# Light units in runs of four, one gather for two light experts, and column halves at the end of an expert

## The chip, the cores and the metric

The kernel runs on one core of one Trainium2 chip. The metric is the device time of one execution in microseconds. A core has TensorE (PE, matmuls; PEld is its weight load), VectorE (DVE), ScalarE (ACT), GpSimd (POOL) and SyncE (SP), and 16 DMA engines that move data between its memory SBUF and HBM. Matmuls write to PSUM, eight banks of 512 float32 columns.

## The reference

Two decoder layers over 256 tokens of width 1024 in float32. Each adds a mixer (differential attention and retention, gated) and then an FFN. In layer 0 the FFN is dense, in layer 1 it is a mixture of eight SwiGLU experts of which each token uses two:

```python
for e in range(N_EXPERTS):
    out = out + combine[:, e:e + 1] * ((silu(t @ w1[e]) * (t @ w3[e])) @ w2[e])
```

with `t = rms_norm(h)`, the top two of the router's logits and a softmax over them for `combine`. An expert's weights are 1024 x 2816 twice and 2816 x 1024: 34.6 MB; all eight 277 MB.

## The kernel before

The weights come as **units** of 128 x 2048 float32 (1.049 MB). The mixers and the dense FFN load them one by one. An expert has 33 units: 22 gate units (`w1` and `w3`; a slice of 512 hidden columns takes four units) and 11 down units (two chunks of 128 hidden rows by 1024 columns each). They are loaded in pairs, 2.1 MB in one DMA, the last one alone: 17 loads per expert, 136 in all (`LOADS`).

**Two kinds of experts.** The experts are put in order of how many tokens they have, counted on the chip. Four places (`CHAIN`) are computed densely for up to 128 tokens: each unit is split by ScalarE (`split_hi`, line 598) and VectorE (`split_lo`, line 616) into a high and a low part, and `product` (lines 621 to 623) makes three matmuls of each tile, 12 per unit with 512 columns. Four places (`SMALL`, the **light** experts, up to 64 tokens) skip the split: `few_halves` (line 1728) multiplies float32 directly, two column halves side by side in the array. A dense unit takes more TensorE time, a light one less, and both bring the same bytes. `moe_orders` mixes the two, so that TensorE and DMA keep step: after each dense load it lets in light loads that are due. `LOADED` is the order of the transfers, `TAKEN` the order of use; a light load is used before the dense load that was fetched just ahead of it. `FEW_ALONE` is the number of light units meant to come after all dense ones.

**The ring.** Loads go to a ring of five places of 2.1 MB. SyncE issues load i when load i-5 has left its place (`load_ring`, line 562, DMAs on lines 578 and 580): a dense one when its last unit is split, a light one when TensorE has used it. Splits run two units ahead of TensorE.

**Gathers.** Tokens of an expert are gathered by matmuls with a one-hot matrix `sel`, made on VectorE (`chain_select`, `few_select`). `gather_rows` (line 1612) does it for a dense expert with 128 places, `few_gather_rows` (line 1624) for one light expert with 64. They read `hn`, the normed rows, which `normed_rows` (line 1104) makes from `xs` on ScalarE just after the first dense unit. Only the first gather (line 1600) reads `xs` and has the norm `rn` in `sel`. Before it `keep_busy_wide` has TensorE multiply spare data, at its end three strided matmuls (line 1547).

**The results.** The rows of each expert but the last light one are stored to HBM in `y_rows` (line 800 and `few_store_rows`). When the last dense rows are stored, GpSimd fetches each token's rows by index (line 825) and VectorE adds them to `h` (`add_rows`, line 2401). The last light expert isn't stored: ScalarE copies its result out of PSUM (line 1189), TensorE spreads it over the tokens (`few_scatter`, line 1796), VectorE adds it (`few_add`, line 2462), and three DMAs write the output (lines 741, 743 and 1247).

Of the kernel before, what the change touches and what calls it, by code (L numbers as in the profile page):

```python
# [31 lines left out]
P = 128  # L32
# [42 lines left out]
FEW_FROM, FEW_ALONE = 6, 12  # L75
# [8 lines left out]
def moe_orders():  # L84
# [97 lines left out]
def build(nc, x, boot_d, positions, units_d, pairs_d, lasts_d, zeros_d, cols_d, rows_d, out):  # L182
    ctx = ExitStack()
    with ctx:
# [27 lines left out]
        few_X = over("few_X", KC * FEW)[:, :].rearrange("p (c n) -> p c n", c=KC)  # L212
# [5 lines left out]
        y_back_rows = over("y_back_rows", D)  # L218
# [10 lines left out]
        back.append(y_back_rows)  # L229
# [10 lines left out]
        raw = sb("raw", [P, RAW, UNIT])  # L240
        wh = sb("wh", [P, SPLIT, UNIT], F32R)
        wl = sb("wl", [P, SPLIT, UNIT], F32R)
# [3 lines left out]
        hn = nc.alloc_sbuf_tensor_at("hn", [P, TT * D], F32, offset=xt_at + 4 * 2 * KC * P)  # L246
# [8 lines left out]
        back.append(cols[:, COLS_LAST:COLS_LAST + D])  # L255
# [151 lines left out]
        y_first = sem("y_first")  # L407
# [21 lines left out]
        hn_rows = sem("hn_rows")  # L429
# [41 lines left out]
        TURNED, FEW_TURNED, FEW_ROWS, FEW_DOWN = 4, 5, 2, 3  # L471
        FEW_SUMS = (0, 1, 6, 7)
# [275 lines left out]
        def _(pool):  # L748
# [47 lines left out]
            def store_rows(p, e):  # L796

                pool.wait_ge(y_cp, 2 * l_no(p) + 2)
                pool.wait_ge(y_sent, 16 + 16 * l_no(p))
                pool.dma_start(rows_in(y_d, Y_ZERO, e), xs3[:, 0, :]).then_inc(y_sent, 16)  # L800

            def few_store_rows(p, e):
# [28 lines left out]
        def _(act):  # L831
# [265 lines left out]
            def normed_rows():  # L1097

                act.wait_ge(rs_ready, 2 * ROOTS)
                for n in range(2):  # L1100
                    act.wait_ge(hg_ready, n + 1)
                    for t in range(TT):
                        at = slice(t * D + n * 512, t * D + (n + 1) * 512)
                        ins = nc.scalar.activation(hn[:, at], xs[:, at], ACT.Copy, scale=rn[:, t:t + 1])
                    ins.then_inc(hn_rows, 1)

# [12 lines left out]
            def few_rows_whole(p):  # L1119

                act.wait_ge(few_rows_tr, few_no(p) + 1)
                nc.scalar.activation(few_X[:, :, :], ps[:, FEW_ROWS, :].rearrange("p (c n) -> p c n", c=KC), ACT.Copy)\
                    .then_inc(few_rows, 1)
# [41 lines left out]
            def few_unit(p, U, j):  # L1165
# [12 lines left out]
                if u == 8 and few_no(p) + 1 < len(SMALL):  # L1178
                    few_rows_whole(SMALL[few_no(p) + 1])
                if u == 6 and p == SMALL[-1]:  # L1180
                    act.wait_ge(few_sel_tr, 1)
                    nc.scalar.activation(selT[:, 0:SEQ], ps[:, TURNED, 0:SEQ], ACT.Copy).then_inc(few_sel_cp, 1)
                if u == SLICES - 1:
                    if few_no(p) > 0:
                        act.wait_ge(few_sent, 32 * few_no(p))
                    act.wait_ge(unit_used, U.count(j))
                    for n in range(2):
                        at = slice(256 * n, 256 * n + 256)
                        nc.scalar.activation(xs3[:, 1, at], ps[:, FEW_DOWN, at], ACT.Copy).then_inc(few_y, 1)

            def large_unit(p, U, j, scatter=None):
# [20 lines left out]
                if then is not None:  # L1212
                    split_hi(act, *then)
                if u == SLICES - 1:
# [3 lines left out]
                    act.wait_ge(y_first, l_no(p) + 1)  # L1218
                    nc.scalar.activation(xs3[:, 0, 0:512], ps[:, banks[0], :], ACT.Copy).then_inc(y_cp, 1)
                    act.wait_ge(unit_used, U.count(j))  # L1220
                    nc.scalar.activation(xs3[:, 0, 512:D], ps[:, banks[1], :], ACT.Copy).then_inc(y_cp, 1)
# [29 lines left out]
        def _(pe):  # L1251
# [243 lines left out]
            def down_unit(pe, U, j, outs, gT, u, halves=None):  # L1495
# [4 lines left out]
                steps = [(a, n) for a in range(2) for n in range(2)]  # L1500
                if halves is not None:
                    steps.sort(key=lambda step: step[1])
                for a, n in steps:
                    b = slice(a * D + n * 512, a * D + (n + 1) * 512)
                    for banks, t in outs:
                        last = product(ps[:, banks[n], :], gT[0][:, 2 * u + a, t], gT[1][:, 2 * u + a, t],
                                       wh[:, s, b], wl[:, s, b], u == 0 and a == 0, u == SLICES - 1 and a == 1)
                    if halves is not None and (a, n) == (1, 0):
                        last.then_inc(halves, 1)
# [28 lines left out]
            def keep_busy_wide():  # L1538
# [47 lines left out]
            def gather(sels):  # L1586
# [3 lines left out]
                of = xs if routing else hn  # L1590
# [1038 lines left out]
```

## Time and profile before

| | |
|---|---|
| median of 3 runs | 1219.03 us (1218.44 to 1220.32) |
| profiled execution | 1219.02 us, its span 1217.2 us |
| busy: PE, DVE, ACT, POOL | 1202.1, 737.4, 593.7, 67.8 us |
| moved by DMA | 384.8 MB |
| expert stage | from about 550 us to the end |

An engine's busy time over the span says how full it is on average, not what sets the end. Times in rows are microseconds from the start of the span. Where several matmuls stand in one row, the duration runs from the first start to the last end, and matmuls overlap: what counts is the distance of the starts.

### The profile page before, as it was taken

The page shows a single profiled execution, that of the slowest core. Times are in us where ns is not written, and L with a number is a line of the kernel's source. Part 1 is how long each engine was busy: PE and PEld are TensorE (multiplying, and loading weights), DVE is VectorE, ACT ScalarE, POOL GpSimd, SP SyncE. Part 2 cuts the span into 40 slices and gives each one's busy share as a digit, 9 for nine tenths or more (in the row PEclk, how much of TensorE's full clock was granted, in tenths as well). Part 3 has the DMA queues.
Part 4 walks back from the last instruction along what each step waited for, and adds up shares of the span by engine and source line. Part 5 has one row for each costly group of instructions (what it writes and reads, how often), then busy time and mean ns, then how long its engine had stood idle before and what let it go on. Part 6 is the DMA issues. An engine that isn't in the chain of part 4 may idle for free.

```text
span 1217.2 us, 15724 instructions
## 1 busy us (share of the span) xinstructions
PE 1202.1 (99%) x6377; PEld 907.8 (75%) x6377; DVE 737.4 (61%) x769; ACT 593.7 (49%) x645; POOL 67.8 (6%) x55
## 2 busy tenths in 40 slices
PE   9999999999999999999999999999999999999996
PEld 8778888888888888888777666777567776667762
DVE  6867766656445857767665745755546664566532
ACT  6667435444436467446545434544535444454430
POOL 0600001000000600000000000000000000000001
PEclk9999999999999999999999999999999999999999
DMA  9753558555554454367999999999999999999997
GB/s 378 302 197 117 182 184 295 184 202 178 184 197 173 169 177 141 136 248 275 408 425 428 385 424 416 428 428 418 424 416 430 427 421 415 427 429 426 429 423 299
DMA packets 36590, 384.82 MB, mean 316 GB/s; under 512 B 4337, under 2 KB 4337, under 8 KB 7985
## 3 DMA queue, kind: packets, MB, share of 16 engines
q1 hardware_dynamic: 34672, 374.83, 76.8%
q0 software_dynamic: 1696, 8.66, 1.9%
q8 instruction: 53, 0.87, 0.3%
q10 hardware_dynamic: 144, 0.26, 0.1%
q14 instruction: 25, 0.20, 0.0%
HBM read 379.80 MB, written 7.61 MB: 318 GB/s over the span
## 4 chain that ended last, share of the span: by engine, by line
PE 91%; DMA 2%; DVE 2%; issue 2%; ACT 1%; POOL 1%; SPq 0%; DVEq 0%; ACTq 0%; POOLq 0%
PE ps L621 22%; PE ps L623 21%; PE ps L622 21%; PE ps L1728 18%; PE ps L1254 3%; DMA ring<-in_pairs 1%; PE ps L1624 1%; DMA h<-in_x 1%; PE ps L1612 1%; DVE wl L616 1%; POOL rst L759 1%; PE ps L1313 1%; ACT wh L598 0%; PE ps L1600 0%; DVE mix L2088 0%
## 5 line engine op out<-in xcount | busy, mean ns | idle before, releaser
L616 DVE TENSOR_TENSOR wl<-raw,wh 128x2048 fp32r<-128x2048 f32 x170 | 391.9, 2307 | 259.8 <-ACT wh L598 259.2
L598 ACT ACTIVATE wh<-raw 128x2048 fp32r<-128x2048 f32 x170 | 325.4, 1917 | 262.5 <-PE ps L623 243.6
L621 PE MATMUL ps<-wh,XT 128*128 128x512 f32 x856 | 341.7, 399 | 1.2 <-DVE wl L616 1.1
L623 PE MATMUL ps<-wh,XT 128*128 128x512 f32 x856 | 333.8, 390 | 0.0
L622 PE MATMUL ps<-wl,XT 128*128 128x512 f32 x856 | 333.6, 390 | 0.0
L621 PEld LDWEIGHTS ps<-wh,XT 128*128 128x128 f32 x856 | 160.7, 188 | 52.2 <-issue 16.2
L623 PEld LDWEIGHTS ps<-wh,XT 128*128 128x128 f32 x856 | 160.7, 188 | 34.5
L622 PEld LDWEIGHTS ps<-wl,XT 128*128 128x128 f32 x856 | 160.9, 188 | 30.9
L616 DVE TENSOR_TENSOR wl<-ring,wh 128x2048 fp32r<-128x2048 f32 x48 | 109.9, 2290 | 79.5 <-ACT wh L598 79.2
L598 ACT ACTIVATE wh<-ring 128x2048 fp32r<-128x2048 f32 x48 | 91.9, 1914 | 101.7 <-PE ps L623 90.8
L1728 PE MATMUL ps<-raw,few_X 128*64 128x256 f32 x768 | 88.2, 382 | 0.0
L1728 PEld LDWEIGHTS ps<-raw,few_X 128*64 128x64 f32 x768 | 53.0, 137 | 31.4 <-issue 7.2
L1728 PE MATMUL ps<-ring,few_X 128*64 128x256 f32 x640 | 73.5, 382 | 0.0
L621 PE MATMUL ps<-wh,moe_gT_h 128*128 128x512 f32 x176 | 71.2, 405 | 0.0
L623 PE MATMUL ps<-wh,moe_gT_l 128*128 128x512 f32 x176 | 68.7, 390 | 0.0
L622 PE MATMUL ps<-wl,moe_gT_h 128*128 128x512 f32 x176 | 68.7, 390 | 0.0
L1728 PEld LDWEIGHTS ps<-ring,few_X 128*64 128x64 f32 x640 | 44.3, 137 | 25.9 <-issue 5.8
L1728 PE MATMUL ps<-raw,few_gT 128*64 128x512 f32 x208 | 48.9, 600 | 0.1
L621 PEld LDWEIGHTS ps<-wh,moe_gT_h 128*128 128x128 f32 x176 | 33.1, 188 | 10.8 <-issue 3.9
L923 ACT ACTIVATE mix<-ps,rn 128x512 f32<-128x512 f32 x40 | 26.0, 688 | 27.2 <-PE ps L623 27.1
L623 PEld LDWEIGHTS ps<-wh,moe_gT_l 128*128 128x128 f32 x176 | 33.0, 188 | 7.2
L622 PEld LDWEIGHTS ps<-wl,moe_gT_h 128*128 128x128 f32 x176 | 33.1, 188 | 6.1
(296 smaller groups left out, 1151.9 us busy)
## 6 DMA issues: line engine op xcount, KB each, us to landing
raw<-in_pairs SPq DMA_DIRECT2D x76, 2048.0 KB, 13.1
ring<-in_pairs SPq DMA_DIRECT2D x52, 2048.0 KB, 13.5
raw<-in_units SPq DMA_DIRECT2D x86, 1024.0 KB, 4.9
raw<-in_lasts SPq DMA_DIRECT2D x6, 1024.0 KB, 13.6
y_rows<-in_zeros POOLq DMA_DIRECT2D x7, 512.0 KB, 7.9
raw<-in_boot SPq DMA_DIRECT2D x5, 512.0 KB, 7.1
y_rows<-xs POOLq DMA_DIRECT2D x4, 512.0 KB, 10.9
ring<-in_lasts SPq DMA_DIRECT2D x2, 1024.0 KB, 10.9
```

Source lines behind the costliest of these rows:

```text
L598: nc.scalar.activation(wh[:, U.split_slot(j), :], U.raw(j), ACT.Copy).then_inc(hi_ready, 1)
L616: nc.vector.tensor_tensor(wl[:, s, :], U.raw(j), wh[:, s, :].bitcast(F32), ALU.subtract).then_inc(lo_ready, 1)
L621: nc.tensor.matmul(o, xh, bh, start=start, stop=False)
L622: nc.tensor.matmul(o, xh, bl, start=False, stop=False)
L623: return nc.tensor.matmul(o, xl, bh, start=False, stop=stop)
L759: nc.gpsimd.tensor_tensor(to, of, nhalf[:, 0:of.shape[-1]], ALU.pow).then_inc(rs_ready, 1)
L923: ins = nc.scalar.activation(to, acc, ACT.Copy if g < 6 else ACT.Sigmoid, scale=rn[:, t:t + 1])
L1254: return nc.tensor.transpose(o, i, ident)
L1313: last = nc.tensor.matmul(ps[:, (6, 6, 4)[k] + c, a * n:(a + 1) * n], qkT[part, hd, tok[t]], qkT[part, 4 + hd, 0:n], start=True, stop=True)
L1612: last = nc.tensor.matmul(ps[:, rows_bank(p) + n, a * P:(a + 1) * P], hn[:, at:at + P], sel[:, t * SEQ:t * SEQ + P], start=t == 0 and a == ...
L1624: last = nc.tensor.matmul(ps[:, FEW_ROWS, c * FEW:(c + 1) * FEW], hn[:, at:at + P], sel[:, t * SEQ + P:t * SEQ + P + FEW], start=t == 0 an ...
L1728: last = nc.tensor.matmul(o[at], x, of[half], start=start, stop=stop, tile_position=(0, half * FEW))
```

## The change

- `moe_orders` lets light loads in two at a time, so that a run of light work is four units (three where an expert's single last unit is among them), and `FEW_ALONE` goes from 12 to 16.
- `few_select` and `few_gather_rows` serve two light experts at once, in 64 of 128 places each; two gathers in place of four.
- `hn` and `normed_rows` are gone. All gathers read `xs`, and `rn` is multiplied into the one-hot matrices. The results that lay in `xs` go to a tile `ys` in the place of `hn`. One split of the opening comes ahead of the first copies of gathered rows on ScalarE.
- The three strided matmuls of `keep_busy_wide` are gone.
- The last two units of each expert hold the last four chunks by column halves, so that one half of the columns is finished a unit earlier. The last light expert uses two PSUM banks, and its copy, spread and add go half by half. `few_store_rows` stores the same rows in pieces of 256 columns.

```diff
-FEW_FROM, FEW_ALONE = 6, 12
+FEW_FROM, FEW_ALONE = 6, 16
...
-        while due - done >= few[0][2]:
-            loaded.append(few[0])
-            taken.insert(len(taken) - 1, few[0])
-            done += few.pop(0)[2]
+        while due - done >= few[0][2] + few[1][2]:
+            for _ in range(2):
+                loaded.append(few[0])
+                taken.insert(len(taken) - 1, few[0])
+                done += few.pop(0)[2]
...
+        FEW_ROWS = (2, 5)
+        FEW_SUMS = ((0, 6), (2, 4))
+        def few_down_banks(p):
+            return (3, TURNED) if p == SMALL[-1] else (3, 3)
...
-                for n in range(2):
-                    pool.dma_start(rows_in(y_d, Y_ZERO, e)[0:FEW, n * 512:(n + 1) * 512],
-                                   xs3[n * FEW:(n + 1) * FEW, 1, 0:512]).then_inc(few_sent, 16)
+                for half in range(2):
+                    to = rows_in(y_d, Y_ZERO, e)[0:FEW, :].rearrange("r (n h d) -> r h n d", n=2, h=2)[:, half]
+                    of = ys[half * FEW:(half + 1) * FEW, 1, 0:512].rearrange("p (n d) -> p n d", n=2)
+                    pool.dma_start(to, of).then_inc(few_sent, 16)
...
-            def normed_rows():
...
-                if (p, j) == (0, 1):
-                    normed_rows()
+            split_hi(act, *ahead_of(units_of(0), 0))
             gathered_hi(0)
...
+            def down_half_unit(pe, U, j, banks, gT, n):
+                pe.wait_ge(lo_ready, U.splits(j))
+                s = U.split_slot(j)
+                for a in range(4):
+                    c, b = FC - 4 + a, slice(a * 512, (a + 1) * 512)
+                    last = product(ps[:, banks[n], :], gT[0][:, c, 0], gT[1][:, c, 0], wh[:, s, b], wl[:, s, b], False, a == 3)
+                last.then_inc(unit_used, 1)
...
-                for _ in range(3):
-                    nc.tensor.matmul(ps[:, 4, :].rearrange("p (t b n) -> p t b n", t=2, n=16), x,
-                                     w.rearrange("p (b t n) -> p t b n", t=2, n=16), start=True, stop=True)
...
             def few_gather_rows(p):
-                pe.wait_ge(hn_rows, 2)
-                pe.wait_ge(few_sel, few_no(p) + 1)
-                for t in range(TT):
-                    for c in range(KC):
-                        at = t * D + c * P
-                        last = nc.tensor.matmul(ps[:, FEW_ROWS, c * FEW:(c + 1) * FEW], hn[:, at:at + P],
-                                                sel[:, t * SEQ + P:t * SEQ + P + FEW], start=t == 0 and c == 0,
-                                                stop=t == TT - 1 and c == KC - 1)
-                last.then_inc(few_rows_tr, 1)
+                pe.wait_ge(few_sel, few_no(p) // 2 + 1)
+                for n in range(2):
+                    for t in range(TT):
+                        for a in range(4):
+                            at = t * D + (4 * n + a) * P
+                            last = nc.tensor.matmul(ps[:, FEW_ROWS[n], a * P:(a + 1) * P], xs[:, at:at + P],
+                                                    sel[:, t * SEQ + P:(t + 1) * SEQ], start=t == 0 and a == 0,
+                                                    stop=t == TT - 1 and a == 3)
+                    last.then_inc(few_rows_tr, 1)
...
+                for n in range(2):
+                    pe.wait_ge(few_y, 2 * len(SMALL) - 1 + n)
+                    for t in range(TT):
+                        for half in range(2):
+                            at = slice(half * FEW, (half + 1) * FEW)
+                            last = nc.tensor.matmul(ps[:, FEW_SUMS[n][t] + half, n * 256:(n + 1) * 256], selT[at, tok[t]],
+                                                    ys[at, 1, n * 256:(n + 1) * 256], start=True, stop=True)
+                        last.then_inc(few_sum[n], 1)
```

## Rows read from the trace of the kernel before

**Rows 1.** The page's busy times over the whole span.
```profile
PE 1202.1 (99%) x6377; PEld 907.8 (75%) x6377; DVE 737.4 (61%) x769; ACT 593.7 (49%) x645; POOL 67.8 (6%) x55
```

**Rows 2.** Stretches: PE, PEld, DVE, ACT, POOL busy, PE clock, DMA share, GB/s.
```profile
660.00:680.00 20.00, 20.00 (x129) 15.18 (x129) 12.09 (x28) 10.46 (x9) 0.00 (x0) 1.00 0.94 384
680.00:700.00 20.00, 19.31 (x89) 12.73 (x85) 13.18 (x24) 8.93 (x9) 0.00 (x0) 1.00 0.99 406
...
800.00:820.00 20.00, 20.00 (x127) 14.68 (x127) 12.80 (x14) 9.24 (x9) 0.00 (x0) 1.00 1.01 429
...
900.00:920.00 20.00, 20.00 (x106) 12.58 (x106) 10.97 (x7) 8.92 (x10) 1.07 (x2) 1.00 0.99 409
...
1000.00:1020.00 20.00, 20.00 (x130) 14.30 (x128) 11.14 (x10) 8.69 (x7) 0.00 (x0) 1.00 0.99 403
```

**Rows 3.** SyncE's waits from 600 to 1190: for whom, us, times, longest.
```profile
SPq L578 <- DVE wl L616: 383.7, 60, 10.7
```

**Rows 4.** The seventeenth load and the last one: issue, and time to landing.
```profile
L578 SPq DMA_DIRECT2D ring<-in_pairs x1: 328/328/328, 610.5 to 610.5; - x1
...
DMA to landing us min/median/max: 12.6/12.6/12.6
...
L580 SPq DMA_DIRECT2D raw<-in_lasts x1: 332/332/332, 1189.0 to 1189.0; - x1
...
DMA to landing us min/median/max: 15.6/15.6/15.6
```

**Rows 5.** Timeline: start, duration, engine, line. One round, and two light loads in succession.
```profile
1150.04 3.67 PE L1728 MATMUL ps<-raw,few_X 128*64 128x256 f32 x32
...
1154.44 0.40 PE L621 MATMUL ps<-wh,moe_gT_h 128*128 128x512 f32 x1
...
1158.53 0.39 PE L621 MATMUL ps<-wh,moe_gT_h 128*128 128x512 f32 x1
...
1159.30 3.67 PE L1728 MATMUL ps<-raw,few_X 128*64 128x256 f32 x32
...
1188.60 3.60 PE L1728 MATMUL ps<-ring,few_gT 128*64 128x512 f32 x16
...
1192.04 3.60 PE L1728 MATMUL ps<-raw,few_gT 128*64 128x512 f32 x16
```

**Rows 6.** Groups on TensorE: the four light and three dense gathers (busy, mean ns).
```profile
L1624 PE MATMUL ps<-sel,hn 128*128 128x64 f32 x128 | 15.0, 276 | 0.0
...
L1612 PE MATMUL ps<-sel,hn 128*128 128x128 f32 x96 | 11.3, 276 | 0.0
```

**Rows 7.** The opening of the expert stage: timeline rows, and TensorE's longest wait.
```profile
545.04 0.89 PE L1547 MATMUL ps<-wh,MT_h 128*128 128x512 f32 x3
...
545.77 0.29 PE L1579 MATMUL ps<-routed,cols 128*128 128x16 f32 x2
...
553.23 2.55 ACT L1104 ACTIVATE hn<-xs,rn 128x512 f32<-128x512 f32 x4
...
PE ps L621 <- DVE wl L616: 0.9, 1, 0.9
```

**Rows 8.** The end: timeline, a row of the chain of waits, and one stretch.
```profile
1184.60 16.16 DMA ring<-in_pairs
...
1192.77 1.05 POOL L825 DMA_INDIRECT back<-y_rows,yidx  x1 [10.13 <-DMA y_rows<-xs]
...
1204.66 1.94 PE L1728 MATMUL ps<-raw,few_gT 128*64 128x512 f32 x8
...
1207.90 1.28 DVE L2401 SCALAR_TENSOR_TENSOR h<-cols,tw,h 128x1024 f32<-128x1024 f32 x1
...
1209.40 2.73 DVE L2462 SCALAR_TENSOR_TENSOR h<-ps,comb,h 128x512 f32<-128x512 f32 x4 [0.22 <-DVE h L2401]
...
1212.16 0.38 ACTq L1247 DMA_DIRECT2D out<-h  x1
...
1204.50:1210.00 5.50, 3.97 (x18) 1.35 (x16) 4.45 (x4) 0.66 (x2) 0.00 (x0) 1.00 0.27 101
```

More of the change, by code:

```diff
@@ L1211, in large_unit @@
                 then = ahead_of(U, j)
-                if then is not None:
+                if then is not None and not (scatter is None and (p, j) == (0, 0)):
                     split_hi(act, *then)
@@ L1493, in dense, with down_unit @@
                         last.then_inc(down_half, 1)
-            def down_unit(pe, U, j, outs, gT, u, halves=None):
+            def down_unit(pe, U, j, outs, gT, u):
                 pe.wait_ge(lo_ready, U.splits(j))
                 s = U.split_slot(j)
[L1500 to L1509, printed above, removed]
+                for a in range(2):
+                    for n in range(2):
+                        b = slice(a * D + n * 512, a * D + (n + 1) * 512)
+                        for banks, t in outs:
+                            last = product(ps[:, banks[n], :], gT[0][:, 2 * u + a, t], gT[1][:, 2 * u + a, t],
+                                           wh[:, s, b], wl[:, s, b], u == 0 and a == 0, u == SLICES - 1 and a == 1)
+                last.then_inc(unit_used, 1)
[5 more added lines that the diff above has]
+                    last = product(ps[:, banks[n], :], gT[0][:, c, 0], gT[1][:, c, 0], wh[:, s, b], wl[:, s, b], False, a == 3)
                 last.then_inc(unit_used, 1)
@@ L1589, in gather @@
                 routing = isinstance(sels, int)
-                of = xs if routing else hn
                 if not routing:
@@ L1593, in gather @@
                 for n in range(2):
-                    pe.wait_ge(*((hg_ready, n + 1) if routing else (hn_rows, n + 1)))
+                    if routing:
+                        pe.wait_ge(hg_ready, n + 1)
                     for t in range(TT):
@@ L1758, in few_down_unit @@
                 j = 2 * SLICES + u
-                pe.wait_ge(few_lo, few_done(p, u // 2))
+                n = u - (SLICES - 2)
+                pe.wait_ge(few_lo, few_done(p, u // 2 if n < 0 else WIDE))
                 pe.wait_ge(*U.landed(j))
-                w = U.raw(j).rearrange("p (a n d) -> p a n d", a=2, n=2)
-                for a in range(2):
-                    last = few_halves(ps[:, FEW_DOWN, :], few_gT[:, 2 * u + a, :], [w[:, a, n] for n in range(2)],
-                                      u == 0 and a == 0, u == SLICES - 1 and a == 1)
+                banks = few_down_banks(p)
+                if u == 0 and p == SMALL[-1]:
+                    pe.wait_ge(y_cp, 2 * len(CHAIN))
+                if n < 0:
+                    w = U.raw(j).rearrange("p (a n h d) -> p a h n d", a=2, n=2, h=2)
+                    for a in range(2):
+                        x, first = few_gT[:, 2 * u + a, :], u == 0 and a == 0
+                        if banks[0] == banks[1]:
+                            o = ps[:, banks[0], :].rearrange("p (n d) -> p n d", n=2)
+                            last = few_halves(o, x, [w[:, a, half] for half in range(2)], first, False)
+                        else:
+                            for m in range(2):
+                                o = ps[:, banks[m], m * 256:(m + 1) * 256]
+                                last = few_halves(o, x, [w[:, a, half, m] for half in range(2)], first, False)
+                else:
+                    w = U.raw(j).rearrange("p (a h d) -> p a h d", a=4, h=2)
+                    for a in range(4):
+                        last = few_halves(ps[:, banks[n], n * 256:(n + 1) * 256], few_gT[:, FC - 4 + a, :],
+                                          [w[:, a, half] for half in range(2)], False, a == 3 and (n == 1 or banks[0] != banks[1]))
                 last.then_inc(unit_used, 1)
@@ L1791, in few_scatter @@
                 pe.wait_ge(y_cp, 2 * len(CHAIN))
[L1792 to L1797 removed]
+                for n in range(2):
+                    pe.wait_ge(few_y, 2 * len(SMALL) - 1 + n)
[5 more added lines that the diff above has]
+                        last.then_inc(few_sum[n], 1)
             gather(1)
@@ L2569, in ffn @@
                 unit([np.concatenate([w1[half * 4 + c][:, at], w3[half * 4 + c][:, at]], 1) for c in range(4)])
-        for c in range(0, FC, 2):
+        for c in range(0, FC - 4 if wide else FC, 2):
             unit([w2[c][:, 0:512], w2[c][:, 512:D], w2[c + 1][:, 0:512], w2[c + 1][:, 512:D]])
+        if wide:
+            for n in range(2):
+                unit([w2[c][:, n * 512:(n + 1) * 512] for c in range(FC - 4, FC)])
     mixer(0)
```

133 lines of the change are left out of this document (61 added, 72 removed).

## The prediction

> **What bounds the kernel now.** I read the page first. TensorE is busy 99% of the span [rows 1], which looks like a TensorE-bound kernel; but ends of matmuls are modelled, so this alone decides nothing. The second view is the table of stretches over the expert stage [rows 2]. What to see there: TensorE is full, and at the same time the 16 DMA engines are full, and the rate never passes about 429 GB/s. The third view, SyncE's own waits, says who paces the loads: SyncE waits for a ring slot nearly all the time [rows 3], so a transfer starts when TensorE (or the split on VectorE) frees a slot. Both engines are thus close to their limit, and the question is which is late at the end.
>
> Landing times settle it. The seventeenth load, issued at 610.5, took 12.6 us and was there at 623.1; the last one, issued at 1189.0, took 15.6 and was there at 1204.6 [rows 4]. Between them lie 230 units of 1.049 MB, at 429 GB/s 2.446 us each: 563 us. The rest of the traffic in that time (four row stores of 0.52 MB, three of 0.26, about 1.5 of the 2.1 MB of the final row gathers, 0.5 MB of instructions) is 4.9 MB or 11.4 us. Full speed would have ended at 1197; the stream came in 7.6 us later. Where that went, the stretches show: 384, 406, 409 and 403 GB/s instead of 429 in four stretches of 20 us are 2.1, 1.1, 0.9 and 1.2 us, 5.3 in sum [rows 2]. All four lie where one expert gives way to the next, that is beside a gather of rows on TensorE. There TensorE frees slots too late and the DMA engines run dry. So the last landing is set by bytes plus the time lost to a late TensorE, and behind it comes a tail of 12.6 us.
>
> **TensorE's saving.** A round of one light and one dense load ran from 1150.04 to 1159.30, 9.26 us [rows 5]. The dense matmuls inside are 18 starts in 4.09 us (1154.44 to 1158.53), 0.227 each, so 24 cost 5.45. Two light units back to back cost 3.44 (1188.60 to 1192.04). The remainder, 0.37 us, is the price of changing between light and dense work, there and back. Writing out both orders gives 59 such rounds before and 29 after (29 runs of four or three light units): 30 x 0.37 = 11.1 us saved. A gather for one light expert (128 matmul records with 64 columns) costs 3.75 us, the one for a dense expert with 128 columns 3.77 [rows 6]; columns do not count here, so one shared gather costs what a single one did, and two of four vanish: 7.5 us. Light units left for after the dense work go from 13 to 19 (loads go in pairs, so sixteen becomes nineteen): 6 x 1.72 = 10.3 us leave the dense stretch. In the opening, three strided matmuls stand ahead of the routing matmuls (0.7 us from their start to that of the next [rows 7]), and the 2.55 us of scaled copies on ScalarE delay a split for which TensorE waits 0.9 us [rows 7]; both go away, the second because rn now sits in the one-hot factors and one split moves into idle time. TensorE would so reach the end of dense work 1.6 + 11.1 + 7.5 + 10.3 = 30 us sooner if data were always there. They are not.
>
> The added operations are cheap. The shared selection is still four VectorE instructions; the copy of shared rows is two ScalarE instructions in place of one; light results now go out in pieces of 1 KB. The last two units of each dense expert hold the same 24 products. The last light expert writes two banks with twice the matmuls at half the columns, the form in which gate units already run at the same 1.72 us. I cost all these at nothing: ScalarE and VectorE do them under a light run of 6.9 us, and uncovered they would cost at most their own length, 0.64 us for 512 columns on ScalarE (2.55 for four [rows 7]), twice.
>
> **What of it reaches the end.** TensorE alone would end the dense work at about 1180 - 30 = 1150. The last dense load lands 19 units (46.5 us) and the last store and the row gathers (2.6 MB, 6.1 us) before the last landing; with that at about 1200, as found below, it is 1147. The two are level now, where before TensorE was the later one. So saved TensorE time pays only where the stream starved or started late. Terms, against the last landing at 1204.6:
> (a) Start. Slots are freed by TensorE's progress. At least its 1.6 us come through. The seventeenth load waits, by the rule of load i-5, for the fourth light load in both orders, with 14 dense and eight light units of work ahead of its slot; the changes on that way fall from 3.5 rounds to 1.5, 0.7 us more. I take 2.3, and twice the 0.7 as the upper bound, 3.1, since the loads in between move too.
> (b) Starvation. Of 5.3 us visible, from nothing to all may come back. The first handover comes after only five rounds, too early for much lead; the later ones find TensorE ahead. I take 3.5.
> (c) Final row gathers. Now they are issued from 1192.8 on [rows 8], in the way of the last two loads, and part of their bytes moves after the last landing: 101 GB/s over 5.5 us from 1204.5 on [rows 8], 0.55 MB. With 19 light units behind the dense work, all is done before. Their bytes then lie ahead of the last load: +1.3 us.
> The last landing moves by -2.3 - 3.5 + 1.3 = -4.5 us.
> The Trainium skill (DMA: Bandwidth & Descriptors, "Issuing engines are not separate DMA queues") says that transfers issued from GpSimd and SyncE share the same 16 DMA engines and interleave. By that rule (c) is a cost, as I take it; with separate paths it would be zero and the sum 1.3 us lower.
>
> (d) Tail. Before: last unit 1204.66 to 1206.60, copy, four sums; VectorE is busy adding gathered rows until 1209.18 and starts the light adds at 1209.40; last store issued 1212.16, and the span ends 5.0 us later [rows 8]. After: the gathered rows are in long before, and the first half of the columns is copied while the second is computed, so the first add starts some 0.6 us behind TensorE's last product instead of 2.8; against this, the last load will land only 2.45 us behind the pair before it (3.8 now: 1184.60 + 16.16 against 1204.6 [rows 4, 8]), whose two units take 3.44, so TensorE ends up to 1.0 us later against the landing. Net 1.2 to 2.2 saved, I take 1.7.
>
> Sum: -4.5 - 1.7 = -6.2 us. The profiled execution took 1219.02, its span 1217.2, the median of the runs is 1219.03, so there is nothing to correct: 1212.8 us.
>
> **The rivals.**
> Starvation stays (0.14): longer runs of light units free two slots at once and then none for a long dense stretch, so the handovers stay as dry as they are. Term (b) is 0, the time 1216.3.
> Lumpy slots starve the stream (0.08, the one on the other side). Each run of four leaves some 11 us of dense work in which slots come free only by splits. Now the queue holds two to three loads (12 to 17 us of landing time at 4.9 each), which speaks against it. If each of the 29 rounds lost 0.3 us of stream, that would be 8.7 us and eat the whole gain; from 0.3 on it is a loss, and with 0.5 the time is 1227.
> More comes back (0.14): all starvation, and the whole 3.1 of the start: -3.1 - 5.3 + 1.3 - 2.2 = -9.3, 1209.7.
> The clock falls (0.04): after the dense work TensorE has 3.44 us of work for each 4.9 us of stream and idles 1.5 us per load, nine times. The granted clock stayed at 1.00 in the stretch from 1204.5 to 1210, although TensorE was busy for only 3.97 of its 5.5 us [rows 8]. If it fell to its lower level, the last unit and sums would take twice their 4 us: 1216.8. The Trainium skill (TensorE: Matmul & The Clock Gate, "What's actually happening") holds that idleness throttles the clock; no row shows it for waits this short.
> The change does nothing (0.04): something else, such as 1 KB store pieces or instruction fetches, takes what was won: 1219.
>
> **Numbers.** The forecast itself has 0.56, own range 1211 to 1215. A measurement of this kernel can tell about 0.2%, 2.4 us. Faster by more: forecast, "more", and six in ten of "starvation stays": 0.78. Within: 0.14. Slower: 0.08. The 8-in-10 range: down to the better case with its bounds, 1209.0, up past "starvation stays" with the weaker tail (1.2) and start (1.6), 1217.5.
>
> **What the profile after should show.** TensorE waiting for DMA several times after the dense work, none of it in the opening; dense work ending between 1148 and 1158; the stretches at the handovers near 425 GB/s; the last landing at about 1200; the row gathers issued near 1165 and added before the last unit; a first light add within 1 us of the last product. The prediction is wrong if SyncE issues fall behind in bursts and stretches below 415 GB/s appear in the steady part, or if TensorE waits on VectorE inside runs of four.

## The result and the profile after

The changed kernel took 1225.09 us in the median of six runs (1221.47 to 1225.4), the kernel before 1218.76 in the six beside it (1218.37 to 1220.32). The ratio is 1.0045, 95% interval 1.0035 to 1.0056: slower by 0.45%, 6.3 us, where 6.2 us less were forecast. The profiled execution is the fastest of the six, 1221.47 us with a span of 1219.8, so its trace shows only part of the loss.

The page's busy times of the kernel after, against [rows 1]:

```profile
PE 1193.2 (98%) x6454; PEld 919.7 (75%) x6454; DVE 738.8 (61%) x765; ACT 593.1 (49%) x641; POOL 68.0 (6%) x55
```

TensorE is busy for 8.9 us less and the kernel is slower: work was taken away, and more waiting came. What the stretches of the kernel after show, in the columns of [rows 2]:

```profile
660.00:680.00 20.00, 19.93 (x120) 14.26 (x118) 14.31 (x34) 10.51 (x9) 0.00 (x0) 1.00 0.96 385
680.00:700.00 20.00, 19.24 (x99) 12.56 (x100) 12.01 (x19) 9.30 (x9) 0.57 (x1) 1.00 0.96 390
...
840.00:860.00 20.00, 15.36 (x89) 9.81 (x88) 6.47 (x6) 4.63 (x5) 0.00 (x0) 0.83 1.00 418
...
900.00:920.00 20.00, 20.00 (x106) 13.68 (x103) 6.83 (x5) 9.30 (x10) 1.12 (x2) 1.00 0.92 359
980.00:1000.00 20.00, 20.00 (x122) 14.64 (x121) 10.63 (x8) 8.68 (x7) 0.00 (x0) 1.00 0.96 387
```

The first handover is as dry as before (385 and 390 GB/s against 384 and 406). The row that stands out is 840 to 860: TensorE is idle for 4.6 us and the granted clock is 0.83. Two stretches behind it, 900 to 920 and 980 to 1000, run at 359 and 387 GB/s.

TensorE's waits of the kernel after, from 600 to 1219 (for whom, us in all, times, longest):

```profile
PE ps L1718 <- DMA raw<-in_pairs: 7.3, 5, 2.5
PE ps L1718 <- DVE few_gbuf L2439: 4.6, 1, 4.6
PE ps L1718 <- DMA ring<-in_pairs: 3.4, 3, 1.8
```

The second is one single wait of a light gate unit on VectorE, inside a run of four. The timeline around it (the dense products are left out; `few_halves` is L1718 now, `split_hi` L603, `split_lo` L621, the light sigmoid L1150, the light gate product L2439):

```profile
842.14 3.67 PE L1718 MATMUL ps<-raw,few_X 128*64 128x256 f32 x32
845.83 1.91 ACT L603 ACTIVATE wh<-raw 128x2048 fp32r<-128x2048 f32 x1 [7.04 <-PE ps L1718]
...
847.65 0.37 ACT L1150 ACTIVATE few_sgm<-ps 128x256 f32<-128x256 f32 x1
847.77 2.29 DVE L621 TENSOR_TENSOR wl<-raw,wh 128x2048 fp32r<-128x2048 f32 x1 [6.66 <-ACT wh L603]
...
849.98 0.42 DVE L2439 TENSOR_TENSOR few_gbuf<-ps,few_sgm 128x256 f32<-128x256 f32 x1
...
850.45 6.46 PE L1718 MATMUL ps<-ring,few_X 128*64 128x256 f32 x32 [4.64 <-DVE few_gbuf L2439]
```

Read it from the bottom. TensorE could not begin light unit (4,20), that is unit 20 of the expert in place 4, because the piece before it had not been gated (a piece is the four gate units of one slice of 512 hidden columns). The gating needs the sigmoid, an instruction of 0.37 us, and that stood on ScalarE behind the split of dense unit (3,0), the first unit of the next dense expert, which began at 845.83. Its releaser is given as TensorE, but the split waits for two things, and the load of that unit tells more. Its issue and its landing:

```profile
L583 SPq DMA_DIRECT2D raw<-in_pairs x1: 341/341/341, 831.1 to 831.1; - x1
...
DMA to landing us min/median/max: 14.7/14.7/14.7
```

831.1 + 14.7 is 845.8. The split waited for bytes that, in the ring's order, were behind those of the light run it held up; VectorE then held the gate product behind its own half of the split for another 2.29 us. I call this the **blocked queue**. It comes from the order: splits run two dense units ahead; where a light run stands ahead of an expert's single last unit, the split issued just before the run is that of the next expert's first load, which is fetched after the run's loads. Written out, the order after has two such places: the runs (2,20) to (2,23) and (4,18) to (4,21). In the second, TensorE needs a gated piece inside the run (unit 20 opens a piece). In the order before there are two as well, (4,22) to (4,23) and (6,20) to (6,21), of one load each and with no piece opening inside.

Behind the wait the same 32 matmuls take 6.46 us in place of 3.67, since the clock is at its lower level, 1.2 GHz:

```profile
849.30:856.10 6.80, 5.65 (x28) 3.19 (x30) 3.83 (x5) 1.17 (x2) 0.00 (x0) 0.50 1.01 429
```

The end of the kernel after:

```profile
1168.49 0.55 POOL L805 DMA_DIRECT2D y_rows<-ys  x1 [76.36 <-ACT ys L1218]
...
1179.00 1.05 POOL L831 DMA_INDIRECT back<-y_rows,yidx  x1 [9.96 <-DMA y_rows<-ys]
...
1194.53 3.67 PE L1718 MATMUL ps<-raw,few_gT 128*64 128x256 f32 x32 [2.46 <-DMA raw<-in_pairs]
...
1200.73 5.36 PE L1718 MATMUL ps<-raw,few_gT 128*64 128x256 f32 x32 [2.16 <-DMA raw<-in_pairs]
...
1210.38 1.93 PE L1718 MATMUL ps<-raw,few_gT 128*64 128x256 f32 x16
...
1213.11 2.73 DVE L2486 SCALAR_TENSOR_TENSOR h<-ps,comb,h 128x512 f32<-128x512 f32 x4 [3.58 <-PE ps L1804]
...
1215.87 0.38 ACTq L1243 DMA_DIRECT2D out<-h  x1
```

The loads of this stretch land 6.2 us apart (TensorE resumes at 1194.53 and 1200.73, each time released by a landing), where a pair at full rate takes 4.89. The last load was issued at 1186.8. The trace doesn't hold its landing, but its last packets end at 1209.1, and in five other traces of this case the landing stands 0.4 to 0.7 us behind the last packet. So it landed at about 1209.5 (an estimate), 5.0 us later than before; from there to the end of the span it is 10.3 us against 12.7.

### The profile page after: what moved, and what is told of

Same layout as the page of the kernel before. It is cut to its first block, busy times and chain, and to the rows that moved or that the text cites. A ratio compares the mean times of both kernels' runs of the same rounds, so it can differ in the third digit from the quotient of the medians.

```text
span 1219.8 us, 15862 instructions
## 1 busy us (share of the span) xinstructions
PE 1193.2 (98%) x6454; PEld 919.7 (75%) x6454; DVE 738.8 (61%) x765; ACT 593.1 (49%) x641; POOL 68.0 (6%) x55
## 4 chain that ended last, share of the span: by engine, by line
PE 83%; DMA 9%; DVE 3%; issue 3%; ACT 1%; POOL 1%; SPq 0%; DVEq 0%; ACTq 0%; POOLq 0%
PE ps L626 20%; PE ps L628 20%; PE ps L627 20%; PE ps L1718 16%; DMA raw<-in_pairs 5%; PE ps L1250 3%; DMA ring<-in_pairs 3%; DVE wl L621 1%; DMA h<-in_x 1%; PE ps L1610 1%; ACT wh L603 1%; POOL rst L764 1%; PE ps L1622 1%; PE ps L1309 1%; PE ps L1599 0%
## 5 line engine op out<-in xcount | busy, mean ns | idle before, releaser
L621 DVE TENSOR_TENSOR wl<-raw,wh 128x2048 fp32r<-128x2048 f32 x162 | 373.2, 2307 | 216.6 <-ACT wh L603 209.9
L603 ACT ACTIVATE wh<-raw 128x2048 fp32r<-128x2048 f32 x162 | 310.3, 1918 | 215.0 <-PE ps L628 160.4
L621 DVE TENSOR_TENSOR wl<-ring,wh 128x2048 fp32r<-128x2048 f32 x56 | 127.9, 2289 | 84.9 <-ACT wh L603 84.9
L603 ACT ACTIVATE wh<-ring 128x2048 fp32r<-128x2048 f32 x56 | 107.3, 1915 | 104.2 <-DMA ring<-in_pairs 52.9
L1718 PE MATMUL ps<-raw,few_X 128*64 128x256 f32 x896 | 102.2, 381 | 2.7 <-DMA raw<-in_pairs 2.7
L1718 PEld LDWEIGHTS ps<-raw,few_X 128*64 128x64 f32 x896 | 63.7, 137 | 36.7 <-issue 8.8
L1718 PE MATMUL ps<-ring,few_X 128*64 128x256 f32 x512 | 61.4, 395 | 5.5 <-DVE few_gbuf L2439 4.6
L1718 PEld LDWEIGHTS ps<-ring,few_X 128*64 128x64 f32 x512 | 37.8, 142 | 26.6 <-issue 6.7
L1718 PE MATMUL ps<-raw,few_gT 128*64 128x256 f32 (+1 forms) x304 | 51.7, 486 | 5.1 <-DMA raw<-in_pairs 4.6
L1718 PEld LDWEIGHTS ps<-raw,few_gT 128*64 128x64 f32 x304 | 23.1, 142 | 27.5 <-issue 22.3
L1150 ACT ACTIVATE few_sgm<-ps 128x256 f32<-128x256 f32 (+1 forms) x24 | 8.6, 360 | 62.4 <-PE ps L1718 62.4
```

Source lines behind the costliest of these rows:

```text
L603: nc.scalar.activation(wh[:, U.split_slot(j), :], U.raw(j), ACT.Copy).then_inc(hi_ready, 1)
L621: nc.vector.tensor_tensor(wl[:, s, :], U.raw(j), wh[:, s, :].bitcast(F32), ALU.subtract).then_inc(lo_ready, 1)
L1718: last = nc.tensor.matmul(o[at], x, of[half], start=start, stop=stop, tile_position=(0, half * FEW))
```

## The experiments

Each kernel is the changed one but for what its text says. The ratios are to the kernel before, run alongside: its medians were 1218.84 (beside e1 to e4), 1218.80 (e5 to e8), 1219.10 (e9 to e11) and 1219.24 (e12). e7 and e11 leave out work that the result needs; they only price it.

| label | median us (lowest to highest) | ratio, 95% |
|---|---|---|
| e1_skip | 1217.50 (1215.98 to 1220.92) | 0.9992 (0.9983 to 1.0001) |
| e2_alone12 | 1216.28 (1215.16 to 1218.98) | 0.9980 (0.9970 to 0.9989) |
| e3_twos16 | 1217.19 (1214.52 to 1218.81) | 0.9986 (0.9977 to 0.9995) |
| e4_twos12 | 1218.47 (1216.05 to 1220.25) | 0.9997 (0.9988 to 1.0006) |
| e5_put_back | 1220.51 (1218.06 to 1223.81) | 1.0014 (1.0005 to 1.0023) |
| e6_spare_work | 1222.67 (1220.81 to 1224.39) | 1.0029 (1.0017 to 1.0042) |
| e7_half_gathers | 1213.74 (1213.30 to 1214.80) | 0.9961 (0.9947 to 0.9974) |
| e8_from4 | 1216.68 (1215.60 to 1217.63) | 0.9981 (0.9972 to 0.9990) |
| e9_split_later | 1217.69 (1216.51 to 1221.02) | 0.9989 (0.9980 to 0.9998) |
| e10_twos12_skip | 1215.44 (1213.98 to 1216.40) | 0.9971 (0.9960 to 0.9982) |
| e11_no_row_gathers | 1212.46 (1211.50 to 1214.01) | 0.9946 (0.9932 to 0.9959) |
| e12_before_skip | 1218.80 (1217.29 to 1219.38) | 0.9992 (0.9983 to 1.0001) |

**The order.** One line more in `moe_orders`, the old constant, the old loop, and both:

```diff
 e1_skip
+        if load[2] == 1:
+            continue
         due = max(0, n - FEW_FROM) * (n_few - FEW_ALONE) // (n_chain - FEW_FROM)
 e2_alone12
-FEW_FROM, FEW_ALONE = 6, 16
+FEW_FROM, FEW_ALONE = 6, 12
 e3_twos16, and with FEW_ALONE 12: e4_twos12
-        while due - done >= few[0][2] + few[1][2]:
-            for _ in range(2):
+        while due - done >= few[0][2]:
+            for _ in range(1):
```

> The changed kernel with one line more in the order: no light run is let in ahead of an expert's single last unit (it comes one dense load later). Theory A, blocked queue: in the changed kernel ScalarE must split a unit of a load that lies behind the two light loads of a run, so the light sigmoid queued behind it waits for that landing, TensorE stands still for 4.6 us at 846, its clock falls for 6.8 us, and the stream starves afterwards in the stretches up to 1000. By A the wait of 4.6 us on VectorE and the clock fall at 849 are gone, the stretch from 900 to 920 is back above 405 GB/s, and the time falls by 6 to 10 us against the changed kernel, to 1212 to 1219. Rival B, the long light end (19 units alone, with the row gathers between the last loads): the wait goes, but the last landing stays within 2 us of 1209 and the time at 1219 to 1224. Rival C, lumpy slots: starvation at the handovers stays as it is, time above 1220.

> The changed kernel with FEW_ALONE back at 12: 15 light units instead of 19 behind the dense work, and by the order written out also no run whose preceding split needs a load behind it. Theory A: as good as the run with the mended order, 1212 to 1219, within 1.5 us of it. Rival B: better than that run by 2 us or more, since the row gathers then collide less with the last loads and TensorE idles less at the end. Rival C: above 1220.

> The changed kernel with light loads let in one at a time as before, FEW_ALONE 16 (17 units alone). Two light runs still stand ahead of a load they need, but no piece of 512 columns ends inside such a run, so the sigmoid isn't needed in it. Theory A: a short wait of some 0.7 us as in the kernel before, no clock fall near 850, time 1213 to 1219. Rival B: the time stays at 1220 or above because the end is as long. Rival C (lumpy slots are the cause): 1216 or below.

> The changed kernel with the order of loads of the kernel before (one light load at a time, FEW_ALONE 12, 13 units alone); what is left of the change are the shared gathers, the opening and the column halves. TensorE has 7.5 + 1.6 us less to do than before and the end is shorter. Theory A: 1213 to 1216. If shared gathers or column halves carry a cost of their own that I have not seen (rival D), it is at 1219 or above.

All four are faster than the changed kernel by 6.6 to 8.8 us, and none has the wait of 4.6 us. With FEW_ALONE 12 the fours fall so that no run stands ahead of a single unit. Twos and fours differ little. e3 still has two runs ahead of a single unit, (2,22) to (2,23) and (4,20) to (4,21), but each is one load, no piece opens behind work of the same run, and its longest wait on VectorE is 0.9 us. e4 missed its range of 1213 to 1216 by 2.5 us and is the slowest of the four: it keeps the order of the kernel before, and there the blocked queue shows in a small form, at run (4,22) to (4,23):

```profile
849.35 1.92 ACT L603 ACTIVATE wh<-raw 128x2048 fp32r<-128x2048 f32 x1 [5.96 <-DMA raw<-in_pairs]
...
851.30 2.29 DVE L621 TENSOR_TENSOR wl<-raw,wh 128x2048 fp32r<-128x2048 f32 x1 [5.58 <-ACT wh L603]
...
854.53 0.30 PE L1250 MATMUL ps<-cols,few_gbuf 128*128 128x128 f32 x1 [1.83 <-DVE few_gT L2453]
854.76 3.28 PE L1718 MATMUL ps<-raw,few_gT 128*64 128x512 f32 x8
```

A wait of 1.83 us, and the eight matmuls behind it take 3.28 us, not 1.94.

**Put it back, take the clock out, and what the first handover costs.** e5 starts from e2 and moves one run ahead of the single unit (1,32) again. e6 starts from the changed kernel. e7 and e8 start from e2.

```diff
 e5_put_back
+        if load[:2] == (CHAIN[1], FFN_UNITS - 3):
+            continue
         while due - done >= few[0][2] + few[1][2]:
...
+            if load[:2] == (CHAIN[1], FFN_UNITS - 1):
+                break
 e6_spare_work
+                if (p, j) == (SMALL[1], 20):
+                    keep_busy(24)
                 if s > 0 and k == 0:
                     pe.wait_ge(few_half, few_done(p, s - 1))
 e7_half_gathers, in gather_rows
-                    for t in range(TT):
+                    for t in range(1):
...
-                                                    stop=t == TT - 1 and a == 3)
+                                                    stop=a == 3)
 e8_from4
-FEW_FROM, FEW_ALONE = 6, 16
+FEW_FROM, FEW_ALONE = 4, 12
```

> The kernel with FEW_ALONE 12 (1216.3 us, no long wait) with one thing put back: the run of light units (4,18) to (4,21) is moved one load later, to just ahead of the single last unit of the second dense expert, as in the changed kernel; the run after it moves along. All else, the number of runs and the fifteen light units at the end, stays. Blocked queue: ScalarE then waits for load 62 with the split of the next dense expert's first unit ahead of the sigmoid of the light piece, TensorE stands 3.5 to 5 us at L1718 on few_gbuf near 846 us, the granted clock may fall to half for 3.4 to 6.8 us behind it, and the median rises by 2 to 6 us, to 1218.3 to 1222. Rival (the place of the run does not matter, the tail of nineteen units and the number of runs did it): 1216.3 within 0.6 us and no such wait.

e5 is 4.2 us slower than e2, in the range given, and the chain of waits of this kernel (start, us, what; lines are four further down) shows the same step with the load itself in it:

```profile
833.67 12.87 DMA raw<-in_pairs
846.56 1.92 ACT wh L607
848.54 2.17 issue
850.71 0.43 DVE few_gbuf L2443
851.18 5.22 PE ps L1722 x32
```

So the place of one run of four light units costs 4.2 us (the run after it moves one load along with it), with the number of runs and the fifteen units at the end the same. The clock fell here too: the 32 matmuls behind the wait took 5.22 us.

> The changed kernel with 24 spare matmuls of ones (0.12 to 0.20 us each by the rows of such matmuls, 3 to 5 us in all) on TensorE just ahead of light unit (4,20), where it stood idle for 4.6 us and the granted clock then was at half for 6.8 us. Theory that the idle time lowers the clock: the granted clock stays at 1.00 there, the wait that is left is under 2 us, the next run of 32 light matmuls takes 3.7 us in place of 6.5, and the median falls by 1 to 3.4 us, to 1221.7 to 1224.1. Rival (the clock falls for another reason, or the 3.4 us are absorbed by the full ring): the clock falls all the same, or it stays up and the median is within 0.6 us of 1225.1.

2.4 us faster than the changed kernel. The stretch that was at 0.83 in the kernel after:

```profile
849.00:856.00 7.00, 6.33 (x58) 5.28 (x58) 5.31 (x5) 4.38 (x5) 0.00 (x0) 1.00 1.02 435
840.00:860.00 20.00, 19.33 (x142) 14.99 (x141) 7.65 (x6) 4.76 (x6) 0.00 (x0) 1.00 1.00 424
900.00:920.00 20.00, 20.00 (x106) 13.56 (x105) 6.70 (x5) 9.17 (x10) 1.11 (x2) 1.00 0.93 365
```

The clock stays up through the same delay, and the light matmuls take 3.67 us. The spare products ran for 5.62 us and a wait of 0.67 was left, so the delay is not shorter, and 900 to 920 stays at 365 GB/s (this profiled execution, 1224.39 us, is the longest of its six). By the medians the clock is thus worth about 2.4 us of the loss, and the delay itself the larger rest. The intervals of the two kernels overlap (1.0017 to 1.0042 and 1.0035 to 1.0056), so the 2.4 is rough. That the clock fell is not a matter of one trace: the granted clock, averaged over an execution, was 0.993 to 0.995 in all six of the changed kernel and 0.995 to 0.998 in the six of e6.

> The kernel with FEW_ALONE 12, with half of each of the three later dense gathers left out: only the first 128 tokens are multiplied in (16 matmuls in place of 32, 1.9 us less on TensorE each time, some 1.9 us just ahead of the first handover). Late TensorE starves the stream: the loads at the first handover that were issued with a nearly empty queue (excess over 4.89 us a pair 1.2, 1.2 and 2.0 us) lose 1 to 2 us of their 4.4 us, and the median falls by 1 to 2 us, to 1214.3 to 1215.3. Rival (slots come free in lumps, or other traffic takes the time): the same excess, median within 0.6 us of 1216.3.

It leaves half of each of three gathers out and is 2.5 us faster than e2. The two stretches of the first handover, e2 ahead of e7:

```profile
660.00:680.00 20.00, 20.00 (x121) 14.44 (x119) 14.09 (x34) 10.72 (x9) 0.00 (x0) 1.00 0.95 382
680.00:700.00 20.00, 20.00 (x105) 13.40 (x105) 13.26 (x19) 9.96 (x10) 0.57 (x1) 1.00 0.97 392
```

```profile
660.00:680.00 20.00, 20.00 (x130) 14.43 (x128) 14.89 (x35) 8.73 (x8) 0.00 (x0) 1.00 1.00 408
680.00:700.00 20.00, 20.00 (x99) 13.48 (x95) 13.26 (x19) 11.22 (x11) 0.57 (x1) 1.00 0.98 396
```

382 and 392 GB/s become 408 and 396, that is (26 + 4) x 20 / 429 = 1.4 us of stream for 1.9 us of TensorE. The late TensorE does starve the stream here. The median fell by 0.5 us more than the upper end given; that part is not settled.

> FEW_ALONE 12 and FEW_FROM 4 in place of 6: the light units begin two units earlier, so that TensorE has about 1 us less to do before the first handover; no light run stands ahead of a single unit. If TensorE's lateness at the first handover starves the stream, up to 1 us less is lost there and the median is 1215.3 to 1216.3; if not, it is 1216.3 within 0.6; if the opening suffers (light rows are needed earlier), it is 1 us slower.

1216.68, 0.4 us from e2: no effect that can be told. Light work two units earlier does not help at the first handover, which ran at 347 and 399 GB/s in this trace.

**Mend the queue without touching the order, and price the gathers.** In e9 the order is that of the changed kernel:

```diff
 e9_split_later, on ScalarE and with split_lo on VectorE
+                late = scatter is None and (p, j) == (CHAIN[1], FFN_UNITS - 2)
-                if then is not None and not (scatter is None and (p, j) == (0, 0)):
+                if then is not None and not late and not (scatter is None and (p, j) == (0, 0)):
                     split_hi(act, *then)
...
+                if (p, j) == (SMALL[1], 19):
+                    split_hi(act, *ahead_of(units_of(CHAIN[1]), FFN_UNITS - 2))
 e10_twos12_skip: the loop of e4 and the two lines of e1
 e11_no_row_gathers, from e2
-                    pool.indirect_dma_start(back[2 * t + a][:, 0:D], None, y_d[:, :], ...
-                dve.wait_ge(y_back[r], 16)
-                stt(h[:, t, :], back[r][:, 0:D], tw[:, 1 + a, t:t + 1], h[:, t, :], ALU.mult, ALU.add)\
+                stt(h[:, t, :], xs[:, t * D:(t + 1) * D], tw[:, 1 + a, t:t + 1], h[:, t, :], ALU.mult, ALU.add)\
```

> The changed kernel, its order of loads and units untouched. Only one split (that of the first unit of the third dense expert, on ScalarE and on VectorE) is issued behind the instructions of light unit (4,19) in place of behind dense unit (1,31), that is behind the sigmoid and the product of the light piece for which TensorE stood 4.6 us. Blocked queue: the wait on few_gbuf near 846 us is gone, the granted clock stays at 1.00 there, and the median falls from 1225.1 by the 4.6 us and the 3.4 us that the clock cost, less what the ring had taken up: to 1217.5 to 1220.5. Rival (the order itself, with nineteen units at the end, costs the time): 1223 or more, with the wait gone.

1217.69: one split, issued behind one light unit more, takes 7.4 us off the changed kernel. The timeline of e9:

```profile
844.45 3.67 PE L1721 MATMUL ps<-raw,few_X 128*64 128x256 f32 x32
847.96 3.62 PE L1721 MATMUL ps<-ring,few_X 128*64 128x256 f32 x32
848.15 3.71 ACT L603 ACTIVATE wh<-raw 128x2048 fp32r<-128x2048 f32 x2 [6.61 <-PE ps L1721]
```

```profile
840.00:860.00 20.00, 18.81 (x117) 13.92 (x117) 9.89 (x8) 9.33 (x9) 0.55 (x1) 1.00 1.01 428
900.00:920.00 20.00, 20.00 (x106) 14.52 (x105) 10.75 (x7) 11.97 (x11) 1.11 (x2) 1.00 1.01 429
```

The two light pairs follow each other without a gap while ScalarE stands waiting for the same late load. Of the wait of 4.6 us one of 1.19 us is left behind the run (at 852.8, for a light product on VectorE). The stretch 900 to 920 is back from 359 to 429 GB/s: the lost stream there was a debt of the stall at 846.

This profiled execution, 1221.02 us, is the slowest of the eleven of e9, hardly below the 1221.47 of the changed kernel's trace. The stall is gone from it all the same, and the last load's packets end at 1205.6, not 1209.1. The rest went at the end, where the granted clock was at its lower level from 1204.3 to 1207.8:

```profile
1203.49 5.36 PE L1721 MATMUL ps<-ring,few_gT 128*64 128x256 f32 x32 [2.49 <-DMA ring<-in_pairs]
...
1208.65 1.93 PE L1721 MATMUL ps<-raw,few_gT 128*64 128x256 f32 x16
```

> The order of the kernel before (runs of two, FEW_ALONE 12) with all else of the change, and no light run ahead of an expert's single last unit. With the single units not skipped it took 1218.5 us, had a wait of 1.8 us on few_gT near 853 and 3.4 us at half clock behind it. Blocked queue: that wait is 0.7 us or less, the clock stays up there, and the median falls by 0.7 to 2.5 us, to 1216.0 to 1217.8. Rival (runs of two are slower for their changes of work, 11 us more TensorE time): 1218.5 within 0.6 us.

1215.44, 3.0 us below e4 and the fastest kernel that computes all; it lies 0.6 us below its range. The longest wait on VectorE is 0.7 us and the clock is full; from 850 to 860 e4 stands ahead of e10:

```profile
850.00:860.00 10.00, 8.17 (x29) 3.34 (x28) 6.29 (x10) 4.10 (x6) 0.00 (x0) 0.83 1.01 428
```

```profile
850.00:860.00 10.00, 9.31 (x44) 4.79 (x44) 6.39 (x10) 4.26 (x7) 0.55 (x1) 1.00 1.01 428
```

The trace of e4 is that of its fastest execution, 1216.05 us, and the one of e10 took 1215.89, so the two show the place and not the 3.0 us. Over all executions the granted clock averages 0.995 to 0.998 in e4 and 0.998 to 0.999 in e10.

The kernel with runs of two is no slower than that with runs of four (e2, 1216.28; the intervals overlap), although TensorE's busy time is 1194.6 us in it and 1189.6 in e2.

> The kernel with FEW_ALONE 12 with the four final row gathers left out, and the four adds of gathered rows on VectorE made on xs in their place. The gathers' 2.1 MB share the DMA engines with the last five loads, four of which took 0.9 to 1.3 us longer than 4.89 for a pair. By their bytes the last landing comes 4.3 to 4.9 us sooner and the median falls to 1211.5 to 1212.5; rival (the longer intervals are those of loads issued late by TensorE): 1216.3 within 1 us.

1212.46, 3.8 us below e2, somewhat less than by the bytes. The stretch 1180 to 1200 shows where the time went, e2 first:

```profile
1180.00:1200.00 20.00, 15.41 (x135) 10.19 (x135) 2.94 (x9) 0.84 (x3) 3.88 (x4) 1.00 1.00 419
```

```profile
1180.00:1200.00 20.00, 17.14 (x151) 11.54 (x151) 6.61 (x12) 0.99 (x4) 0.00 (x0) 1.00 0.88 373
```

With the gathers the DMA engines are full (1.00) and TensorE gets its weights later (15.41 us busy); without them TensorE is busier and the engines run out of work before 1200. The gathers share the engines with the loads. That is what the Trainium skill (DMA: Bandwidth & Descriptors, "Issuing engines are not separate DMA queues") states, and the runs agree.

**Is it the order alone?**

```diff
 e12_before_skip, on the kernel before
+        if load[2] == 1:
+            continue
```

> The kernel before with one thing alone: no light run ahead of an expert's single last unit (runs of two, FEW_ALONE 12, none of the rest of the change). The version of the change with this order took 1215.4 us. If its gain is the earlier start and the shorter end (2.0 and 0.6 to 1.4 us by the landings), the order alone brings nothing here, as TensorE waited no longer than 0.7 us at those places in the kernel before: 1218.2 to 1219.4. If the order brings it, 1216 to 1217.5.

1218.80 beside 1219.24: nothing that can be told from no change. In the kernel before TensorE never waited over 0.7 us at these places, so e10's gain is the rest of the change, once nothing stands in its way.

## Why the prediction was wrong

**The failing step.** The sum has no term for TensorE waiting on ScalarE or VectorE inside a run. "I cost all these at nothing: ScalarE and VectorE do them under a light run of 6.9 us" is its only word on the two engines; it looked at how much work they have (there, the added operations), not at what their queues stand behind. What stood in its place is a wait of 4.6 us and what followed from it. Two effects of the change meet: a run has two loads, so that a piece opens inside it, and the shift by FEW_ALONE 16 puts such a run ahead of a single unit. The prediction named TensorE waiting on VectorE inside runs of four as what would make it wrong, and gave it neither a place nor a price. Moving one run into the place costs 4.2 us (e5 against e2), taking one split out of the way in the changed kernel gives back 7.4 (e9). The kernel with the stall loses in three steps: the wait of 4.6 us, the half clock behind it (about 2.4 us of the median, e6), and a TensorE so late that the stream starves further on. At 429 GB/s the stretches 900 to 920 and 980 to 1000 lose 5.2 us in the changed kernel and 1.3 in e9, so 4.0 go with the stall; in e5 the stall takes 2.2 in the same way (900 to 920 and 1000 to 1020, 398 and 399 GB/s against 428 and 417 in e2). Why the debt is smaller there stays open. Starvation stayed, as its rival had it, in the kernels with a free queue mostly at the first handover. The rival of lumpy slots had the right side, but not this mechanism: with runs of four and a free queue (e2) the time falls.

**TensorE's saving** was put at 30 us. The shared gathers came out as costed: 7.6 us busy for 64 matmuls in place of 15.0 for 128. The changes between kinds of work did not. e10 and e2 have 57 and 30 runs ahead of dense loads, and differ in TensorE's busy time by 5.0 us, so a round costs 0.19 us (an estimate), half of the 0.37 taken. The dense work ended near 1167, not at 1148 to 1158. With the same order and no light run ahead of a single unit (e1) it ended near 1162: TensorE stood idle for 6.8 us between 562 and that moment, against 1.4 before, and 4.4 of it were waits for loads inside the dense stretch.

**(a) Start, -2.3.** TensorE's wait on `wl` in the opening is gone, and the load holding the twentieth unit landed about 2 us sooner. The seventeenth load, from which the term was worked out, landed 0.6 to 1.7 us sooner (1.3 in the changed kernel and in e2, 0.8 in e1, 0.6 in e4, 1.7 in e10); in e12, whose opening is that of the kernel before, it landed 1.9 us later. By the seventieth unit, behind the first handover, the profiled executions stood between 2.3 us ahead of the kernel before (e4) and 0.7 behind it (e8); e2 and e10 were 0.3 behind. A lead won ahead of a stretch in which TensorE sets the pace need not come through; by how much it does varies too much between executions to be sized here.

**(b) Starvation, -3.5.** Mis-sized. In e2, free of stalls, the two later handovers run at 428 (900 to 920) and 417 GB/s (1000 to 1020): of the 0.9 and 1.2 us, 1.5 come back. The first one, with 3.2 of the 5.3 us, gives back nothing (382 and 392 GB/s, 3.9 us lost; e12, whose loads there are those of the kernel before, lost 3.9 too). The prediction had the reason in it, "too early for much lead", and took 3.5 all the same.

**(c) Row gathers, +1.3.** Right in kind. All four cost 3.8 us of the median (e11). In e2 the last three loads land 5.7, 6.2 and 3.7 us after the one ahead of them in place of 4.9, 4.9 and 2.4, 3.4 us in sum; in the kernel before 5.3, 5.7 and 3.8, or 2.6: +0.8 for the 1.3 taken. Over the last five loads it is 4.5 against 3.3, +1.2, and 5.1 or +1.7 in e1, which has nineteen units at the end as the changed kernel has. In the changed kernel the gathers were issued at 1179, not 1165: GpSimd waited 10 us for its last store.

**(d) Tail.** Right: in e2 it is 11.2 us from last landing to end against 12.7, 1.5 less for the 1.7 taken; in e1 it is 1.0 less. In the changed kernel it is 2.4 less, and its first light add came 0.8 us behind the last product.

**The sum.** With the queue free and the order of the change kept (e9), or kept but for the runs ahead of single units (e1), what is left of the -6.2 us is -1.4 and -1.3. Other orders do better: -2.6 with FEW_ALONE 12 (e2), -3.7 with runs of two besides (e10). So even without the blocked queue the forecast was too high. In e2 the largest part missing is (b), 0.8 us by the stretches for the 3.5 taken, then (a); in e1 (c) is larger as well. These parts are read from one execution each and are rough. What was added in the changed kernel is the blocked queue.

## What to carry to other kernels

Work that runs ahead on an in-order engine must not stand ahead of work that the current stage needs, unless its own data lands first: for each item issued ahead, compare the place of its load in the transfer order with that of the work issued behind it. A constant that shifts an interleaving is a change of every such pair, so write out both orders and look for the pairs that turn around. An engine with idle time can still be the one that stops the kernel (here VectorE, busy 61% of the span, and ScalarE, 49%), and a stretch that starves may be paying for a stall 60 us earlier.

## What the runs showed of the hardware

**Short waits lower TensorE's clock, in some executions.** After a wait of 4.64 us the clock was at its lower level for 6.8 us (the kernel after), after 4.84 us light work took 5.22 us in place of 3.67 (e5), after 1.83 us 3.28 in place of 1.94 (e4). With waits of the same length at the end, the kernel after fell in 1200 to 1204 and e2 did not (granted clock 1.00 from 1180 to 1200, where it waited 1.65 and 2.53 us). e6 shows that the idle time is the cause: the same delay, filled with matmuls, keeps 1.00. The prediction had given this 0.04 and looked for it at the end. There it cost nothing in the changed kernel, where the unit of 5.36 us at 1200.73 was done before the next load landed, and about 1.7 us in e9 (an estimate: 5.36 against 3.67 at 1203.49), where the stream was over before that unit ended. The Trainium skill (TensorE: Matmul & The Clock Gate, "What's actually happening") says that the clock is throttled when TensorE is idle, and that the number of matmuls at the lower clock differs from run to run of the same kernel; these traces agree with both.
